# Attention's end marks, half sums and weight split, and the order of values in the retention head

## The reference

```
h = x @ w_in                                   # (tokens, 1024) @ (1024, 10240)
qa, ka, va, za, qr, kr, vr, zr, ga, gb = split(h)
# A: attention, 3 groups (window, dilation) = (128,1), (512,4), (2048,16), 4 heads of 128, ALiBi
s = q . k * scale - slope * dist ; o_a = softmax over the three groups' keys . v
# B: retention, 4 heads, key 128, value 256, chunks of 128
qr, kr = rotary(qr), rotary(kr) * 128 ** -0.5
att = (qc . kc) * dmat ; o = att . vc + (qc . S) * q_decay ; S = chunk_decay * S + (kc * k_decay) . vc
o_r = group_norm(o) * gn_g
out = (sigmoid(ga) * ((silu(za) * o_a) @ w_pa) + sigmoid(gb) * ((silu(zr) * o_r) @ w_pb)) @ w_o
y = layer_norm(alpha * x + out)
```

## Time and profile before

| | us |
|---|---|
| median of 3 runs (lowest, highest) | 854.59 (853.1, 855.23) |
| profiled execution, own time | 854.84 |
| its span | 853.1 |
| TensorE busy | 822.1 (96%) |
| VectorE busy | 485.0 (57%) |
| GpSimd busy | 352.4 (41%) |
| ScalarE busy | 231.5 (27%) |

### The profile page before, as it was taken

The page is one execution under the profiler, slowest core; times in us unless marked ns, Lnnn a source line. Parts: engine busy times, 40 slices in busy tenths (PEclk is TensorE's granted clock), DMA queues, the critical chain, the costliest instruction groups (busy, mean ns, idle before and its releaser), DMA issues.

```text
span 853.1 us, 19281 instructions
## 1 busy us (share of the span) xinstructions
PE 822.1 (96%) x7268; PEld 788.7 (92%) x7268; DVE 485.0 (57%) x839; ACT 231.5 (27%) x334; POOL 352.4 (41%) x261
## 2 busy tenths in 40 slices
PE   7999999999999999997898999999999999999996
PEld 6999999999999999997887888898899999999996
DVE  4367854787377854786454556555573333333467
ACT  5123421343032422440221321212162222222200
POOL 0069953898179934998520524215100000000003
PEclk8999999999999999999999999999999999999999
DMA  7998989769995989595939579396999888888942
GB/s 215 267 270 274 270 267 232 280 140 309 235 267 180 288 253 278 196 216 164 341 109 376 209 273 391 134 375 230 353 307 303 281 276 279 289 296 291 350 152 111
DMA packets 176203, 220.28 MB, mean 258 GB/s; under 512 B 9440, under 2 KB 153824, under 8 KB 174368
## 3 DMA queue, kind: packets, MB, share of 16 engines
q1 hardware_dynamic: 171072, 206.18, 77.2%
q0 software_dynamic: 4432, 11.15, 4.1%
q10 hardware_dynamic: 656, 2.36, 0.7%
HBM read 206.81 MB, written 100.14 MB: 360 GB/s over the span
## 4 chain that ended last, share of the span: by engine, by line
PE 64%; POOL 17%; DMA 7%; issue 6%; DVE 4%; SPq 1%; POOLq 0%; ACT 0%; DVEq 0%; ACTq 0%
PE bank L811 17%; PE bank L813 17%; PE bank L812 17%; POOL far L682 7%; DMA cslot<-in_cache_kv_w_dram 4%; PE bank L841 4%; PE bank L806 3%; POOL prod L682 2%; DMA out_dram<-st 2%; DVE wl L1515 1%; POOL far L685 1%; PE bank L936 1%; PE bank L1108 1%; PE bank L911 1%; POOL prod L685 1%
## 5 line engine op out<-in xcount | busy, mean ns | idle before, releaser
L811 PE MATMUL bank<-xh,wh 128*128 128x288 f32 x640 | 192.6, 301 | 0.1
L811 PE MATMUL bank<-wh,xh 128*128 128x256 f32 x640 | 185.1, 289 | 4.4 <-DVE qk L1742 4.1
L813 PE MATMUL bank<-xh,wl 128*128 128x288 f32 x640 | 189.0, 295 | 0.0
L812 PE MATMUL bank<-xl,wh 128*128 128x288 f32 x640 | 188.9, 295 | 0.0
L812 PE MATMUL bank<-wl,xh 128*128 128x256 f32 x640 | 180.0, 281 | 0.0
L813 PE MATMUL bank<-wh,xl 128*128 128x256 f32 x640 | 179.9, 281 | 0.0
L1515 DVE TENSOR_TENSOR wl<-raw,wh 128x1024 fp32r<-128x1024 f32 (+1 forms) x104 | 155.5, 1533 | 9.1 <-ACT wh L1320 8.3
L811 PEld LDWEIGHTS bank<-wh,xh 128*128 128x128 f32 x640 | 122.1, 191 | 8.6 <-DVE qk L1742 5.2
L682 POOL TENSOR_TENSOR far<-far,qrow 128x1024 f32<-128x1024 f32 x48 | 126.1, 2637 | 0.0
L1320 ACT ACTIVATE wh<-raw 128x1024 fp32r<-128x1024 f32 (+1 forms) x104 | 102.3, 1019 | 79.8 <-PE bank L841 40.9
L811 PEld LDWEIGHTS bank<-xh,wh 128*128 128x128 f32 x640 | 120.8, 189 | 1.9 <-DVE vn L1587 1.0
(11 more groups left out here) (214 smaller groups left out, 1507.9 us busy)
## 6 DMA issues: line engine op xcount, KB each, us to landing
raw<-in_w_in_dram SPq DMA_DIRECT2D x128, 256.0 KB
out_dram<-in_cache_kv_w_dram SPq DMA_DIRECT2D x32, 1020.0 KB, 10.2
cslot<-in_cache_kv_w_dram SPq DMA_DIRECT2D x24, 1024.0 KB, 8.7
out_dram<-in_cache_kv_w_dram SPq DMA_DIRECT2D x12, 2040.0 KB, 10.4
far<-in_cache_kv_w_dram SPq DMA_DIRECT2D x64, 256.0 KB, 7.0
out_dram<-in_cache_kv_w_dram SPq DMA_DIRECT2D x20, 504.0 KB, 8.6
far<-in_cache_kv_w_dram SPq DMA_DIRECT2D x16, 512.0 KB, 6.9
raw<-in_w_in_dram SPq DMA_DIRECT2D x16, 512.0 KB
```

The source lines that it names most:

```text
L811: pe.matmul(out, lhs[0](k), rhs[0](k), start=(k == 0), stop=False)
L812: pe.matmul(out, lhs[0](k), rhs[1](k), start=False, stop=False)
L813: last = pe.matmul(out, lhs[1](k), rhs[0](k), start=False, stop=(k == n - 1))
```

## The change

There are two groups of edits. In stage A: the mark `a_end` is raised by two engines instead of four, VectorE (which takes over GpSimd's waits for the stores) and ScalarE; VectorE copies unit 0 of stage B ahead of its three memsets; four of the ten half sums a head go (those of `middle(1)` and `middle(3)`), and `far_sum(2)`, `(3)` stand behind the softmaxes; the second half of the split `low(c + 4)` stands behind the copy of query unit 15. In stage B: value unit 3 stands ahead of the rotation's turns, `cached_output(0)` ahead of the sample scores, `cached_output(1)` behind query-key units 3 and 4, and the split `low(C0_B + 3)` behind `projected(4)`; SyncE issues the second pair's slots ahead of the next weights and state; keys are turned ahead of the first sample values.

```diff
@@ SyncE, stage_b
                 rows(1, A_COPY_B - 1, r * 126, 126)
+                near_values(r, 1)
+                far_values(r, 1)
+                settle(sp)
+                own_values(r, 1)
                 if not last:
                     retention_chunk(r * B_CH + (C0_B + 3), r + 1, 1)
                     sp.wait_ge(st_stored, r * 64 + 64)
                     settle(sp)
                     states(r + 1)
-                near_values(r, 1)
-                far_values(r, 1)
-                settle(sp)
-                own_values(r, 1)
@@ GpSimd, cached_keys
-                    product(prod[:, :, :], m, 0, k > 0)
-                    product(far[:, m:m + FAR_PIECE, :], m, 1, k > 0)
+                    product(prod[:, :, :], m, 0, k == 2)
+                    product(far[:, m:m + FAR_PIECE, :], m, 1, k == 2)
...
-            pool.wait_ge(k_stored, H * 96)
-            pool.wait_ge(v_stored, H * 128)
-            pool.sem_inc(a_end, 1)
-            pool.wait_ge(a_end, 4)
+            pool.wait_ge(a_end, 2)
@@ TensorE
             qk_unit(0, 0, 0)
-            for b in range(2):
-                pe.wait_ge(tg_free[b], TB_B + 1)
-            pe.matmul(bank[7][:, 0:1], ident, ident[:, 0:1], start=True, stop=True).then_inc(a_end, 1)
...
                 cached_probs(0)
+                value_unit(3)
                 pe.wait_ge(rot_done, r + 1)
...
-                value_unit(3)
+                cached_output(0)
                 sample_att()
...
                 turn_keys(r, 1)
+                cached_turn(0)
                 sample_state_pair(0)
                 value_unit(4)
                 sample_state_pair(2)
-                cached_output(0)
                 att_group()
-                cached_turn(0)
                 state_group(0)
...
                 next_unit(2)
-                cached_output(1)
                 next_unit(3)
                 next_unit(4)
+                cached_output(1)
                 pe.wait_ge(normed, r + 1)
...
+            turn_keys(0, 0)
             sample_values(0, 0)
-            turn_keys(0, 0)
@@ ScalarE, retention_head
+                high(C0_C if last else r * B_CH + (C0_B + 2), 0, used_b(5))
+                cached_output(0)
                 group(3, krt[:, :], bank[7][:, :])
-                high(C0_C if last else r * B_CH + (C0_B + 2), 0, used_b(5))
                 key_copy(r, 1)
-                cached_output(0)
@@ VectorE
-                    if 2 <= n < 12:
+                    if 4 <= n < 10:
                         src = src[:, :, 0:DH // 2]
...
-                low(c + 4, 0)
+                low(c + 4, 0, halves=(0,))
                 queries(15, 2, 1)
-                far_sum(2)
-                far_sum(3)
+                low(c + 4, 0, halves=(1,))
...
             dve.wait_ge(tg_free[1], TB_B + 1)
+            dve.wait_ge(k_stored, H * 96)
+            dve.wait_ge(v_stored, H * 128)
+            dve.wait_ge(unit_done, UD + U_B + 1)
+            dve.wait_ge(far_summed, FAR_PIECES * (H + 1))
             dve.sem_inc(a_end, 1)
-            dve.wait_ge(a_end, 4)
-            dve.wait_ge(gn_in, 16)
-            dve.memset(qm[:, :], 0.0)
-            dve.memset(bank[4][:, :], 0.0)
-            dve.memset(pm[:, :], 0.0).then_inc(cleared, 1)
+            dve.wait_ge(a_end, 2)
...
             projected(0, 0, 0)
+            dve.wait_ge(gn_in, 16)
+            dve.memset(qm[:, :], 0.0)
+            dve.memset(bank[4][:, :], 0.0)
+            dve.memset(pm[:, :], 0.0).then_inc(cleared, 1)
             low(C0_B + 1, 1)
...
                 next_projected(2)
-                if not last:
-                    low(r * B_CH + (C0_B + 3), 1)
                 normalise()
                 next_projected(3)
                 next_projected(4)
+                if not last:
+                    low(r * B_CH + (C0_B + 3), 1)
```

More of the change, by code:

```diff
@@ L557, in _ @@
             retention_chunk(C0_B + 1, 0, 1)
-            sp.wait_ge(a_end, 4)
+            sp.wait_ge(a_end, 2)
             keys(0, 0)
@@ L722, in _ @@
             with pool.Fori(0, H) as h:
-                own.enter(h, 10)
+                own.enter(h, 6)
                 cached_keys(h)
             own.leave(H)
-            pool.wait_ge(k_stored, H * 96)
-            pool.wait_ge(v_stored, H * 128)
-            pool.sem_inc(a_end, 1)
-            pool.wait_ge(a_end, 4)
+            pool.wait_ge(a_end, 2)
             own.after(pool.memset(qk[NS:P, QBLK, :], 0.0))
@@ L1458, in retention_head @@
                     key_copy(r, 2)
-            act.wait_ge(a_end, 4)
+            act.wait_ge(a_end, 2)
             act.wait_ge(kd_done, 1)
@@ L1682, in attention_head @@
                 softmax(0)
+                far_sum(2)
                 za(1)
                 softmax(1)
+                far_sum(3)
                 values(18)
@@ L1880, in retention_head @@
                 normalise_rows(0)
+                values(2)
                 probs(0)
@@ L1889, in retention_head @@
                     .then_inc(rt_free[0], 1)
-                values(2)
+                values(3)
                 b = group(1)
@@ L1895, in retention_head @@
                    qdec.to_broadcast([P, QBLK, P]), ALU.mult).then_inc(rt_free[1], 1)
-                values(3)
                 b = group(2)
@@ L1899, in retention_head @@
                 sample_output()
+                output(0)
                 sample_states(0)
@@ L1906, in retention_head @@
                 attention()
-                output(0)
                 chain(0)
```

## The result

The changed kernel took 868.9 us (median of 4 runs, 861.7 to 872.48) against 854.17 of the kernel before in the same comparison. The ratio is 1.017, with a 95% interval of 1.0144 to 1.0196: it is slower by 1.7%, where 846.0 was predicted. Its runs also lie further apart than those of before (10.8 us against 2.1). The profiled execution is the slowest of the four, 872.48 us with a span of 870.8, so it shows the damage at its largest.

What follows compares the result with a forecast made beforehand. TensorE was taken as the bound, busy 822.1 us of a span of 853.1. Savings of 2.0 + 2.7 + 4.1 = 8.8 us off 854.84 gave 846.0 us, with a range of 842.0 to 850.5.

Steps and rivals of the forecast that it cites:

- part 2: End of attention: chain ends 4.2 us earlier, less 1.5 for half clock behind a 3.7 us gap; 2.7 us won.
- two lock waits of 1.1 left: Last head of attention: GpSimd's last six products lose only 2.2 us to VectorE's weight split, ending at 394.9.
- I take nothing: Attention: the longer far sums give VectorE some 2 us more a head, counted as no cost.
- part 1: Attention, weight split in halves: TensorE's wait for query unit 15 goes, 0.65 us in three heads, 2.0 us won.
- a split that waits for two pieces: Retention heads, split beside the rotation: upper bound of 1.7 us a head if it waits for two GpSimd pieces.
- part 3: Retention heads: waits worth 8.7 us go, new waits of 3.3 and 1.3 come; 4.1 us won.
- the rival of the late values: Retention heads: cached values land too late, 7.1 us in three heads, giving 867 us; chance 0.06.
- the four waits of 0.83 us at `att_group()`: Retention heads: TensorE waits for VectorE's sum, queued behind a weight split; 0.8 us in four heads, 3.3 lost.
- The term of 1.3 us for the split beside the rotation: Retention heads: weight split alternates with GpSimd's rotation, 0.4 us late in three heads; lower bound 0.

Runs made afterwards that it cites:

- e2: Changed kernel, six half sums still out, with GpSimd waiting for its own count behind each of the last six products of a head; 842.14 us, ratio 0.9876.
- e12: Changed kernel with GpSimd waiting for its own count only behind the first product of `middle(3)`; 842.82 us, ratio 0.987.
- e3: Kernel before with only the four half sums a head removed, order and marks as before; 871.34 us, ratio 1.0211.
- e7: e2 with ScalarE's wait for `kd_done` moved one line later, behind its weight split of chunk `C0_B + 1`; 836.08 us, ratio 0.9799.
- e8: e7 with the second half of the weight split `low(C0_B + 2)` of each retention head moved behind `chain(1)`; 836.12 us.
- e4: Kernel before with only the new order in the retention heads; 850.29 us, ratio 0.9971.
- e5: Changed kernel with GpSimd waiting for its own count only behind the second product of `middle(3)`; 853.13 us, ratio 0.9984.

## Why the prediction was wrong

**The step that failed** is in part 2: "while a GpSimd product and VectorE's subtraction of the weights are both in flight they run one after the other", read as turns, so that a split half waits for one product at most ("two lock waits of 1.1 left"). Only e2, e12 and the kernels with half sums behave so. Without a pause on GpSimd the half stands behind all six products, 13.7 to 14.0 us (e3 and the changed kernel against e2, shown). The prediction's range ended at 850.5; these stalls and the clock behind them carried the kernel to 868.9. The rows I had could not tell the two apart, since in the kernel before every product near a split was followed by a half sum; I priced the half sums as GpSimd's work alone and never asked what their waits gave to others. The same holds for "I take nothing" for VectorE in part 1: the price was a term for VectorE's load, and the cost was in its access. No rival had it. I had bounds for a split that waits for two pieces (part 3), and none for a row of six. That the rival of the late values names 867, close to the measured time, is chance: its wait for `cslot` is in no trace of the new order.

The Trainium skill, SBUF — State Buffer, "Summary: rules for kernel authors", says that when a VectorE instruction with two SBUF inputs meets a GpSimd instruction that reads SBUF, the second one to issue fully blocks until the first finishes. That agrees for one pair (the product of 3.22 us behind the half in e12, 2.37 undisturbed). The words "until the first finishes" don't hold for the row: the measured half was passed over by five further products.

**The rest of part 2** held in the main. With pauses, from the start of the first of the six products to the end of the last, e2 takes 16.47 us (372.67 to 389.14); the prediction's 378.4 to 394.9 is 16.5. Unit 3 starts 8.64 us behind the last sum (390.57 to 399.21). Counted from the first row of `on` in head 3, it starts 27.8 us behind that row in e2 and 31.5 us in the kernel before: 3.7 us won, where I had 4.2. One wait of 3.95 us stood ahead of it, predicted 3.7, with the clock at 0.50 behind it. e7 leaves up to 1.7 for that clock, predicted 1.5.

**Part 1** was too small where it worked. The stretch from a row of `on` in head 1 to the same row in head 2, first in the kernel before, then in e2:

```profile
189.03:283.28 94.25, 93.47 (x738) 91.47 (x737) 64.08 (x98) 29.72 (x39) 66.86 (x44) 1.00 0.88 243
```

```profile
185.99:278.70 92.71, 92.71 (x739) 91.64 (x737) 65.35 (x98) 29.82 (x39) 61.21 (x40) 1.00 0.87 246
```

A head is 1.54 us shorter. I had taken the 0.65 a head that the list of waits gives for `qt` (2.6 in the earlier trace rows). With TensorE's instructions of the two stretches set side by side, 0.9 us of the 1.54 is won at `scores(0)` (256.37 us before, 252.10 in e2), which is the term of the prediction, a third larger than the list had it. The rest is won at places that the sum did not have: 0.4 at `output(3)` (199.39 and 196.09), where the split `low(c + 6)` ahead of it takes 5.68 instead of 6.09 us, and 0.2 to 0.3 each at a unit of the next head (207.64 and 204.09) and at the first unit of `zr` (278.81 and 274.16); about 0.2 is lost again in small steps.

**Part 3**: the four waits of 0.83 us at `att_group()` have the predicted size for a wrong reason (e8): not VectorE's queue, only its 0.70 us of reading. The term of 1.3 us for the split beside the rotation was nothing, its lower bound. VectorE came first there and kept both halves (after the change, head 0):

```profile
484.34 2.35 DVE L1509 TENSOR_TENSOR wl<-raw,wh 128x1024 fp32r<-128x1024 f32 x2
...
484.60 3.49 POOL L744 TENSOR_TENSOR rot<-qk,con 128x640 f32<-128x640 f32 x1 [6.51 <-DVE qk L1740]
```

There the product stood behind a row of two. The late values (rival four) did not come.

**In sum**: with the starvation taken out (e2), the change gives 842.1 us, 3.9 below the forecast of 846.0. Three heads of 1.54 instead of 0.65 us make 2.7 of it, and the 1.3 that were not there about the rest. The starvation costs 26.8 us on top.

**Open**: why the runs of the changed kernel spread over 10.8 us. That which heads are starved varies with the arrival of cache data fits heads 0 and 1 and e3's trace, but only one execution of each kernel has a trace.

## What to carry to other kernels

Before removing a small instruction between large ones on GpSimd, look at what VectorE does beside it: a wait of some hundredths of a microsecond between two GpSimd instructions can be VectorE's only way in, and one such wait, near the start of the row, was enough here for a split of two instructions. When two engines share something, read how long the loser stood in the worst row, not only in the usual one, and give the rival "it stands behind the whole row" a price. When an idle gap is explained by a chain, ask of each wait in that chain whether it protects anything that follows it directly: one line moved in e7 gave 6.1 us, more than the whole retention edit (2.8 by e4's medians).

## What the hardware showed that was not expected

A waiting VectorE subtraction with two inputs in SBUF (1.21 us by itself) was not let in between GpSimd products that followed each other directly; it took 13.83 and 13.98 us behind six and 4.56 to 4.75 behind two. A pause of GpSimd (0.08 us by the starts and ends in e5: 385.73 to 385.81) let it in.

The next subtraction then got in behind one product without any pause, in all heads of e5 and e12 (3.38 to 3.40 us each, one product and itself). That the product had itself been held up is not the condition: in the kernel before a subtraction also gets in behind half sums that nothing had held up (1.29 us). In all traces it goes by whether the GpSimd instruction ahead began behind a pause (105 places against 24, under e2). Why that decides is not shown; the traces show only when.

The clock also fell behind waits shorter than the prediction thought it would take: 0.50 (1.2 GHz) behind 1.78 and 2.11 us (the stretches from 107.20 and 202.80), where the prediction counted on 3.7. It isn't fixed by the length alone, since e3's waits of 1.63 to 1.79 us in heads 0 to 2 left it whole (the stretch behind the first, 106.40 to 110.00, was granted 1.00); what decides there stays open. The Trainium skill, TensorE: Matmul & The Clock Gate, "Why this matters for your kernels", warns of idle gaps between bursts of matmuls, but of longer ones than these; these two rows differ from it.

The list of waits undercounts a short stall of TensorE: at `scores(0)` 0.65 us a head by the list, 0.9 by where the instructions behind it moved. Stalls shorter than its smallest rows it does not show at all: some 0.6 us a head were won at three places that it does not name.
